# A dense feed-forward with the roles of its two operands exchanged, in a two-block transformer kernel

## The chip, the cores and the metric

One core of one Trainium2 chip runs the whole program in one launch. The metric is device time in microseconds, from the first to the last instruction and what lies around them. All numbers are float32. The core has five engines that run side by side and meet at semaphores: TensorE (PE) multiplies matrices into PSUM, VectorE (DVE) and ScalarE (ACT) do elementwise work, GpSimd (POOL) some more of it, and SyncE (SP) issues most of the DMAs.

## The reference, cut to what matters

The input is one sequence of 256 tokens of width 1024. It goes through a first block (attention and an RWKV group, then a mixture of 32 small experts) and a second block of two layers. The change is in the feed-forward of the first of these two layers:

```
def swiglu(h, w1, w3, w2):
    return (jax.nn.silu(h @ w1) * (h @ w3)) @ w2
...
for i in range(DEPTH_2):                       # 2 layers
    ...                                        # pool and conv mixer, w_out
    x = layer_norm(DEEPNORM_ALPHA * x + mix, ln1_g[i], ln1_b[i])
    if i % 2 == 0:
        f = swiglu(x, dense_w1[j], dense_w3[j], dense_w2[j])       # 1024 -> 2816 -> 1024
    else:
        f = moe_swiglu(x, router_w[j], exp_w1[j], exp_w3[j], exp_w2[j])   # 8 experts, 2 per token
    x = layer_norm(DEEPNORM_ALPHA * x + f, ln2_g[i], ln2_b[i])
    x = x + jax.nn.sigmoid(x @ ple_gate_w[i]) * (p[i] @ ple_w[i])
```

## The kernel before

Tokens stand in two tiles of 128 rows (TT = 2). Each engine has one instruction stream, written out by hand in program order; the lists in STEPS name the points at which an engine raises its semaphore, and `ba`, `bd` and `bp` turn such a name into a wait on ACT's, DVE's or PE's list.

Weights stream through `ring`, seven places of 2 MB. SP issues one piece after another in a fixed order; piece n waits until `used`, a count that PE raises as it finishes with pieces, shows piece n-7 read. So the order of the pieces must be the order in which PE finishes with them. `has(n)` is PE's wait for piece n. After the dense pieces come those of the per-layer gate (PLE: ple_w and two of ple_gate_w), of the second layer's mixer and of its experts.

A matmul loads a block of 128 columns as the stationary side and moves up to 512 columns of the other operand past it. In the trace a float32 matmul is two pairs of a weight load (LDWEIGHTS) and a MATMUL instruction, so all counts of the trace are twice those of the code; a transposing matmul is one pair.

The dense feed-forward cuts the 2816 middle columns into units of 512, 512, 512, 512, 512 and 256 (UD). For a unit u and a token tile t:

- L1540: w1, 8 matmuls. The stationary side is a 128-token block of `xT` (the input, transposed before), the weights move, 512 columns at a time. The result has tokens in rows.
- L1547: w3, the same, into PSUM bank 2.
- L958 on ACT: silu of the w1 result into `hs`. L2178 on DVE: the product with the w3 result into `hh`.
- L1528: four transposes of `hh` into PSUM bank 3, since the next product needs the middle columns in rows. L2181 on DVE: copy into `hT`.
- L1518: w2, 8 matmuls per tile: `hT` is stationary and w2 moves, 512 columns at a time, summed over all units in PSUM banks 4 to 7.

The order on PE is: w1 of (u, t), the transposes of the step before, w3 of (u, t), w2 of the step before. After the last step the transposes and w2 of (5, 1) stand alone. Then DVE adds the sum to x (L2185) and normalizes, and the gate stage follows (L1468, L1479, L1292, L1497), and the second mixer, which begins with L1400. That stage, and the first mixer before, already use the other form: weight columns are stationary and the whole `xT`, 256 tokens wide, moves (L1400 and, in the first block, L1023).

The eight experts of the second layer run as a loop on PE with two bodies, one for experts with few tokens (two halves of the array) and one for the others; a value read at run time picks one.

Of the kernel before, what the change touches and what calls it, by code (L numbers as in the profile page):

```python
# [10 lines left out]
ALU = mybir.AluOpType  # L11
ACT = mybir.ActivationFunctionType
# [3 lines left out]
P = 128  # L16
D = 1024
S = 256
TT = S // P
KD = D // P  # L20
# [56 lines left out]
class Steps:  # L77
# [12 lines left out]
    def __call__(self, name):  # L90
# [71 lines left out]
    ],  # L162
# [13 lines left out]
def build(nc, x, positions, g_mix, w_in, g_cq, w_uq, g_ckv, w_uk, w_uv, g_qn, g_kn, g_mla_out, rw_mu, rw_w0, rw_w2,  # L176
# [4 lines left out]
    with ExitStack() as ctx:  # L181
# [13 lines left out]
        xT = sb("xT", [P, KD, S])  # L195
        work = sb("work", [P, 14368])
        c_sb = sb("c_sb", [P, TT, C_W])
        ident = sb("ident", [P, P])
# [14 lines left out]
        ps = ctx.enter_context(nc.psum_tensor("ps", [P, 8, 512], F32))  # L213

        def cut(base, at, *shape):

            n = int(np.prod(shape))
            v = base[:, at:at + n]
            names = "abcde"[:len(shape)]
            if len(shape) == 1:  # L220
                return v
            return v.rearrange(f"p ({' '.join(names)}) -> p {' '.join(names)}", **dict(zip(names[1:], shape[1:])))
# [86 lines left out]
        mean, var = tiny(16), tiny(16)  # L309
# [14 lines left out]
        hs = cut(work, 1792, 2, 512)  # L324
        hh = cut(work, 2816, 2, 512)
        hT = cut(work, 3840, 4, P)
        yg = cut(work, 4352, D)
        RT = 7480
        at_rt = [RT]

# [10 lines left out]
        diffs, w2 = rt(2, 5), rt(2, 2)  # L341
# [16 lines left out]
        up = cut(work, 0, NPC, 16 + S)  # L358
# [49 lines left out]
        def place(n):  # L408

            at = (n + 1) % PLACES * PLACE  # L410
            return ring[:, at:at + PLACE]
# [4 lines left out]
        def chunked(v, width):  # L416
            return v[:, 0:KD * width].rearrange("p (k n) -> p k n", k=KD)


        def ffn_order(units):  # L420

            order = []
            for u in range(units):
                order += [("w1", u), ("w3", u)] + ([("w2", u - 1)] if u else [])
            return order + [("w2", units - 1)]
# [1 line left out]
        MIX = [("in", 1), ("in", 2), ("in", 0), ("pw", 0), ("out", 0), ("out", 1)]  # L427
        PLE = [("ple", 0), ("pg", 0), ("pg", 1)]

        DENSE = [(what, u) for u in range(len(UD)) for what in ("w1", "w3", "w2")]  # L430
        MOE = ffn_order(UNITS)
        MIX0, DENSE0 = 0, len(MIX)
        PLE0 = DENSE0 + len(DENSE)
# [12 lines left out]
        def read_dense(what, u):  # L446
            return read(DENSE0 + DENSE.index((what, u)))

# [8 lines left out]
        def _(sp):  # L457
# [85 lines left out]
            for n, (what, u) in enumerate(DENSE):  # L543
                f0, f = 512 * u, UD[u]
                if what == "w2":
                    src = dense_w2_2[0][f0:f0 + f, :].rearrange("(p c) n -> p c n", p=P)
                else:
                    src = (dense_w1_2 if what == "w1" else dense_w3_2)[0].rearrange("(p k) f -> p k f", k=KD)[:, :, f0:f0 + f]
                piece(DENSE0 + n, src)
# [148 lines left out]
        def _(act):  # L698
# [252 lines left out]
            mixer_act(0)  # L951
            turned_x(0, "ffn 0")
            for u in range(len(UD)):
                for t in range(TT):
                    act.wait_ge(*(bp(f"up {u}") if t == 0 else read_dense("w3", u)))
                    if u > 0:
                        act.wait_ge(*bd(f"hidden {u - 1} {t}"))
                    ba.raise_by(act.activation(hs[:, t, 0:UD[u]], ps[:, t, 0:UD[u]], ACT.Silu), f"silu {u} {t}")  # L958
            tail_act(0)
            mixer_act(1)  # L960

# [31 lines left out]
        def _(pe):  # L993
# [387 lines left out]
            def has(n):  # L1381

                pe.wait_ge(landed[(n + 1) % PLACES], 16 * (n // PLACES + 1))
# [122 lines left out]
            turn_x(x_sb, bp, "xT ffn 0", lambda t: [bd(f"ln1 0 {t}")])  # L1506
            pe.wait_ge(*ba("xT ffn 0 3"))

            def dense_down(u, t):
                n_c = UD[u] // P  # L1510
                n2 = DENSE0 + DENSE.index(("w2", u))
                if t == 0:
                    has(n2)
                pe.wait_ge(*bd(f"hT {u} {t}"))
                w = place(n2)[:, 0:n_c * D].rearrange("p (c n) -> p c n", c=n_c)
                for n in range(2):
                    for c in range(n_c):
                        ins = mm(ps[:, 4 + 2 * t + n, :], hT[:, c, :], w[:, c, n * 512:(n + 1) * 512], start=(u == 0 and c == 0),  # L1518
                                 stop=(u == len(UD) - 1 and c == n_c - 1))
                if t == 1:  # L1520
                    ins.then_inc(used, 1)

            def dense_turn(u, t):
                n_c = UD[u] // P
                pe.wait_ge(*bd(f"hidden {u} {t}"))
                v = hh[:, t, 0:UD[u]].rearrange("p (q c) -> p c q", c=n_c)
                for c in range(n_c):
                    ins = turn_(ps[:, 3, c * P:(c + 1) * P], v[:, c, :], ident[:, :])  # L1528
                bp.raise_by(ins, f"hT {u} {t}")

            before_ = None
            for u in range(len(UD)):
                n1, n3 = DENSE0 + DENSE.index(("w1", u)), DENSE0 + DENSE.index(("w3", u))
                has(n1)
                has(n3)
                for t in range(TT):
                    if u > 0:
                        pe.wait_ge(*ba(f"silu {u - 1} {t}"))
                    for k in range(KD):
                        ins = mm(ps[:, t, 0:UD[u]], xT[:, k, t * P:(t + 1) * P], chunked(place(n1), UD[u])[:, k, :],  # L1540
                                 start=(k == 0), stop=(k == KD - 1))
                    if t == 1:
                        ins.then_inc(used, 1)
                    if before_:
                        dense_turn(*before_)
                    for k in range(KD):
                        ins = mm(ps[:, 2, 0:UD[u]], xT[:, k, t * P:(t + 1) * P], chunked(place(n3), UD[u])[:, k, :],  # L1547
                                 start=(k == 0), stop=(k == KD - 1))
                    if t == 0:
                        bp.raise_by(ins, f"up {u}")  # L1550
                    else:
                        ins.then_inc(used, 1)
                    if before_:
                        dense_down(*before_)
                    before_ = (u, t)
            dense_turn(*before_)
            dense_down(*before_)
            ple_pe(0, PLE0, False)
            mixer_pe(1, MIX1)

# [130 lines left out]
        def _(dve):  # L1691
# [10 lines left out]
            def mark(stage, ins, name):  # L1702

                stage.raise_by(ins, name)
                dve.wait_ge(*stage(name))
# [467 lines left out]
            mixer_dve(0)  # L2173

            for u in range(len(UD)):
                for t in range(TT):
                    dve.wait_ge(*ba(f"silu {u} {t}"))
                    mark(bd, tt(hh[:, t, 0:UD[u]], hs[:, t, 0:UD[u]], ps[:, 2, 0:UD[u]], ALU.mult), f"hidden {u} {t}")  # L2178
                    dve.wait_ge(*bp(f"hT {u} {t}"))
                    n_c = UD[u] // P  # L2180
                    mark(bd, cp(hT[:, 0:n_c, :].rearrange("p c s -> p (c s)"), ps[:, 3, 0:UD[u]]), f"hT {u} {t}")  # L2181
            dve.wait_ge(*read_dense("w2", len(UD) - 1))
            for t in range(TT):
                x_t = x_sb[:, t, :].rearrange("p (b n) -> p b n", b=2)
# [111 lines left out]
```

## Time and profile before

| | |
|---|---|
| median of 3 runs | 2221.1 us (2213.69 to 2238.5) |
| profiled execution, its own time | 2220.31 us |
| its span | 2218.5 us |
| PE busy | 1920.7 us, 87% of the span |
| DVE, ACT, POOL busy | 506.2, 240.7, 65.5 us |
| mean granted TensorE clock | 0.94 of full speed |
| HBM read | 543.50 MB, 245 GB/s over the span |

The profiled execution lies 0.8 us under the median, and 1.8 us of it lies outside the span. Times in the trace are from the span's start.

### The profile page before, as it was taken

To read this page: it belongs to the slowest core of one execution; us is meant where nothing else is said; L and a number is where in the kernel's file an instruction comes from. 1 tells how busy PE (TensorE), PEld (TensorE's weight loads), DVE (VectorE), ACT (ScalarE), POOL (GpSimd) and SP (SyncE) were. 2 spreads that over 40 slices of the span, in tenths; PEclk is the share of its full clock that TensorE was granted. 3 is DMA by queue.
4 is the path that set the end of the run, shared out by engine and by line. 5 is a ranking of instruction groups with operands and counts; after the bars stand their busy time and mean duration, and the time that the engine had idled before them with its cause. 6 is when DMAs were issued, how large, how long until landed. Compare 5 with 4: busy or idle time off the path is not lost.

```text
span 2218.5 us, 23585 instructions
## 1 busy us (share of the span) xinstructions
PE 1920.7 (87%) x10059; PEld 1121.5 (51%) x10060; DVE 506.2 (23%) x828; ACT 240.7 (11%) x418; POOL 65.5 (3%) x141
## 2 busy tenths in 40 slices
PE   3967867777878999989779999999799999998877
PEld 2846754554664444548454454455444445544443
DVE  1356621111472000037321000011111001110102
ACT  1242101111211000012110000000000000010001
POOL 3000100000020000001000000000000000000000
PEclk9977869999988999999879999999899999999999
DMA  7040128999733351454127867879999888999990
GB/s 269 1 192 2 40 81 360 402 389 413 276 114 114 114 189 57 168 187 147 38 92 283 296 243 287 294 281 405 393 404 396 313 295 323 397 402 398 402 362 19
DMA packets 169984, 545.75 MB, mean 246 GB/s; under 512 B 6521, under 2 KB 9698, under 8 KB 148146
## 3 DMA queue, kind: packets, MB, share of 16 engines
q1 hardware_dynamic: 166640, 538.33, 63.7%
q0 software_dynamic: 1664, 5.05, 0.7%
q8 instruction: 65, 1.06, 0.2%
q10 hardware_dynamic: 1602, 1.19, 0.2%
q14 instruction: 13, 0.11, 0.0%
HBM read 543.50 MB, written 1.05 MB: 245 GB/s over the span
## 4 chain that ended last, share of the span: by engine, by line
PE 71%; DVE 13%; DMA 8%; issue 3%; ACT 2%; SPq 2%; ACTq 0%; DVEq 0%
PE ps L1611 20%; DMA ring<-in_exp_w 7%; PE ps L1629 7%; DVE work L2137 5%; PE ps L1635 4%; PE ps L1540 4%; PE ps L1518 3%; PE ps L1547 3%; PE ps L1573 3%; PE ps L1328 3%; PE ps L1342 3%; PE ps L1497 3%; PE ps L1455 2%; PE ps L1023 2%; SPq L564 2%
## 5 line engine op out<-in xcount | busy, mean ns | idle before, releaser
L1611 PE MATMUL ps<-ring,work 128*64 128x256 f32 (+1 forms) x2912 | 563.5, 438 | 33.1 <-DMA ring<-in_exp_w 21.6
L1611 PEld LDWEIGHTS ps<-ring,work 128*64 128x64 f32 (+1 forms) x2912 | 282.4, 148 | 298.4 <-issue 183.7
L1635 PE MATMUL ps<-ring,work 128*64 128x512 f32 x560 | 136.0, 631 | 18.9 <-DMA ring<-in_exp_w 10.0
L1629 PE MATMUL ps<-ring,work 128*128 128x512 f32 x336 | 147.8, 593 | 4.6 <-DVE work L2241 4.6
L2241 DVE COPY work<-ps 128x512 f32<-128x512 f32 x56 | 38.7, 690 | 430.6 <-PE ps L1619 430.6
L2235 DVE TENSOR_TENSOR work<-work,ps 128x512 f32<-128x512 f32 x56 | 38.5, 688 | 341.6 <-PE ps L1611 341.6
L975 ACT ACTIVATE work<-ps 128x512 f32<-128x512 f32 x56 | 33.5, 598 | 682.1 <-PE ps L1611 682.1
L1629 PEld LDWEIGHTS ps<-ring,work 128*128 128x128 f32 x336 | 63.6, 190 | 84.0 <-issue 84.0
L2137 DVE SCALAR_TENSOR_TENSOR work<-work,c_sb 128x256 f32<-128x256 f32 x180 | 98.8, 549 | 6.4
L1635 PEld LDWEIGHTS ps<-ring,work 128*64 128x64 f32 x560 | 41.6, 144 | 94.0 <-issue 75.5
L1400 PE MATMUL ps<-xT,ring 128*128 128x256 f32 x384 | 85.8, 387 | 1.1 <-ACT xT L898 1.1
L1400 PEld LDWEIGHTS ps<-xT,ring 128*128 128x128 f32 x384 | 74.6, 195 | 12.4 <-issue 1.9
L1540 PE MATMUL ps<-ring,xT 128*128 128x512 f32 (+1 forms) x192 | 80.2, 572 | 0.7 <-ACT xT L898 0.7
L1328 PE MATMUL ps<-work,xn 128*128 128x128 f32 x256 | 63.3, 425 | 20.1 <-DVE work L2072 20.1
L1518 PE MATMUL ps<-ring,work 128*128 128x512 f32 x176 | 77.6, 593 | 0.6 <-DVE work L2181 0.6
L1547 PE MATMUL ps<-ring,xT 128*128 128x512 f32 (+1 forms) x192 | 77.6, 557 | 0.0
L1573 PE MATMUL ps<-work,xn 128*128 128x128 f32 x288 | 70.3, 405 | 5.8 <-DVE work L2217 5.8
L1573 PEld LDWEIGHTS ps<-work,xn 128*128 128x128 f32 x288 | 69.5, 334 | 11.0 <-DVE work L2217 5.9
L1328 PEld LDWEIGHTS ps<-work,xn 128*128 128x128 f32 x256 | 61.8, 336 | 26.1 <-DVE work L2072 26.1
L1342 PE MATMUL ps<-ring,work 128*32 128x256 f32 x1024 | 58.6, 387 | 11.2 <-DVE work L2076 11.2
L1540 PEld LDWEIGHTS ps<-ring,xT 128*128 128x128 f32 x192 | 37.3, 195 | 42.2 <-issue 40.4
L1497 PE MATMUL ps<-ring,xT 128*128 128x512 f32 x128 | 56.0, 595 | 2.9 <-ACT xT L898 2.9
(463 smaller groups left out, 1682.2 us busy)
## 6 DMA issues: line engine op xcount, KB each, us to landing
ring<-in_exp_w SPq DMA_DIRECT2D x168, 2048.0 KB, 14.5
ring<-in_w_gate SPq DMA_DIRECT2D x32, 1024.0 KB, 8.6
ring<-in_w_up SPq DMA_DIRECT2D x32, 1024.0 KB, 15.4
ring<-in_w_down SPq DMA_DIRECT2D x32, 1024.0 KB, 17.9
ring<-in_dense_w SPq DMA_DIRECT2D x15, 2048.0 KB, 8.1
ring<-in_w_in SPq DMA_DIRECT2D x6, 2048.0 KB, 11.0
ring<-in_w_in SPq DMA_DIRECT2D x8, 1104.0 KB, 16.8
ring<-in_w_out SPq DMA_DIRECT2D x4, 2048.0 KB, 15.4
```

Source lines behind the costliest of these rows:

```text
L1328: ins = mm(ps[:, k // 4, (k % 4) * P:(k % 4 + 1) * P], by8(xn[:, t, :])[:, k, :], ga_sel[:, t, :], start=(t == 0), stop=(t == TT - 1))
L1342: ins = mm(ps[32 * j:32 * j + 32, 2, n * F1:(n + 1) * F1], xg[:, k, 32 * j:32 * j + 32], ring[:, at + k * F1:at + (k + 1) * F1], start=(k ...
L1400: ins = mm(ps[:, bank, half * S:(half + 1) * S], w[:, k, i * P:(i + 1) * P], xT[:, k, :], start=(k == 0), stop=(k == KD - 1))
L1497: ins = mm(ps[:, 2 * t + n, :], xT[:, k, t * P:(t + 1) * P], wg[k // 4][:, k % 4, n * 512:(n + 1) * 512], start=(k == 0), stop=(k == KD - 1))
L1518: ins = mm(ps[:, 4 + 2 * t + n, :], hT[:, c, :], w[:, c, n * 512:(n + 1) * 512], start=(u == 0 and c == 0), stop=(u == len(UD) - 1 and c = ...
L1540: ins = mm(ps[:, t, 0:UD[u]], xT[:, k, t * P:(t + 1) * P], chunked(place(n1), UD[u])[:, k, :], start=(k == 0), stop=(k == KD - 1))
L1547: ins = mm(ps[:, 2, 0:UD[u]], xT[:, k, t * P:(t + 1) * P], chunked(place(n3), UD[u])[:, k, :], start=(k == 0), stop=(k == KD - 1))
L1573: ins = mm(ps[:, 6 + k // 4, (k % 4) * P:(k % 4 + 1) * P], by8(xn[:, t, :])[:, k, :], ga_sel[:, t, :], start=(t == 0), stop=(t == TT - 1))
L1611: ins = mm(ps[cols_j, bank, 0:fh], xg[:, k, cols_j], w[:, k, :, n_c * j:n_c * (j + 1)], start=(k == 0), stop=(k == KD - 1), **tile)
L1629: ins = mm(ps[:, 4 + n, :], hT[:, c, :], w[:, c, n * 512:(n + 1) * 512], start=(first and c == 0), stop=(final and c == 3))
L1635: ins = mm(ps[rows_n, 4 + n, :], hT[:, c % 2, side(c // 2)[0]], w[:, c, n * 512:(n + 1) * 512], start=(first and c == 0), stop=(final and ...
L2137: ins = stt(yv[:, j, :], vp[:, j, tap:tap + S], cw[:, tap, j:j + 1], yv[:, j, :], ALU.mult, ALU.add)
```

## The change

The first two products of the dense feed-forward are turned round. For each chunk of 128 middle columns, the 128 columns of w1 (then of w3) are the stationary side and `xT`, all 256 tokens, moves. The result has the middle columns in rows and is what w2's product takes as its stationary side, after silu and the product. So the transposes on PE and the copies on DVE are gone. ACT and DVE work once per unit, on both tiles together (up to 1024 elements per partition). The PSUM banks are 0 and 1 for w1, 2 and 3 for w3, 4 to 7 for the sum. `hT_d` has two buffers, and w2 of unit u-1 comes after w3 of unit u. The pieces are therefore read in another order, that of `ffn_order` (w1 0, w3 0, w1 1, w3 1, w2 0, w1 2, w3 2, w2 1, and so on, w2 5 last), and w2's rows are laid out as (c p) instead of (p c): a partition now gets four separate rows of 4 KB where it had 16 KB in one run.

```
-        DENSE = [(what, u) for u in range(len(UD)) for what in ("w1", "w3", "w2")]
+        DENSE = ffn_order(len(UD))
...
-                    src = dense_w2_2[0][f0:f0 + f, :].rearrange("(p c) n -> p c n", p=P)
+                    src = dense_w2_2[0][f0:f0 + f, :].rearrange("(c p) n -> p c n", p=P)
...
-                for t in range(TT):
-                    act.wait_ge(*(bp(f"up {u}") if t == 0 else read_dense("w3", u)))
-                    if u > 0:
-                        act.wait_ge(*bd(f"hidden {u - 1} {t}"))
-                    ba.raise_by(act.activation(hs[:, t, 0:UD[u]], ps[:, t, 0:UD[u]], ACT.Silu), f"silu {u} {t}")
+                act.wait_ge(*read_dense("w1", u))
+                if u > 0:
+                    act.wait_ge(*bd(f"hidden {u - 1}"))
+                n_b = UD[u] // 256
+                ba.raise_by(act.activation(hs_d[:, 0:2 * UD[u]].rearrange("p (b n) -> p b n", b=n_b), ps[:, 0:n_b, :], ACT.Silu),
+                            f"silu {u} u")
...
+            def dense_up(what, u, b):
+                n = DENSE0 + DENSE.index((what, u))
+                has(n)
+                w = chunked(place(n), UD[u])
+                for c in range(UD[u] // P):
+                    for k in range(KD):
+                        ins = mm(ps[:, b + c // 2, (c % 2) * S:(c % 2 + 1) * S], w[:, k, c * P:(c + 1) * P], xT[:, k, :],
+                                 start=(k == 0), stop=(k == KD - 1))
+                ins.then_inc(used, 1)
+
+            def dense_down(u):
+                ...
+                has(n2)
+                pe.wait_ge(*bd(f"hidden {u}"))
+                for t in range(TT):
+                    for n in range(2):
+                        for c in range(n_c):
+                            ins = mm(ps[:, 4 + 2 * t + n, :], hT_d[:, u % 2, c, t * P:(t + 1) * P], w[:, c, n * 512:(n + 1) * 512],
+                                     start=(u == 0 and c == 0), stop=(u == len(UD) - 1 and c == n_c - 1))
+                ins.then_inc(used, 1)
...
             for u in range(len(UD)):
...
+                if u > 0:
+                    pe.wait_ge(*ba(f"silu {u - 1} u"))
+                dense_up("w1", u, 0)
+                if u > 0:
+                    pe.wait_ge(*bd(f"hidden {u - 1}"))
+                dense_up("w3", u, 2)
+                if u > 0:
+                    dense_down(u - 1)
+            dense_down(len(UD) - 1)
...
+                dve.wait_ge(*ba(f"silu {u} u"))
+                dve.wait_ge(*read_dense("w3", u))
+                n_b = UD[u] // 256
+                mark(bd, tt(hT_d[:, u % 2, 0:2 * n_b, :].rearrange("p (b c) s -> p b (c s)", b=n_b),
+                            hs_d[:, 0:2 * UD[u]].rearrange("p (b n) -> p b n", b=n_b), ps[:, 2:2 + n_b, :], ALU.mult),
+                     f"hidden {u}")
```

## Rows read from the trace of the kernel before

**Rows 1.** The page: the span, and the chain that ended last, by engine

```profile
span 2218.5 us, 23585 instructions
PE 1920.7 (87%) x10059; PEld 1121.5 (51%) x10060; DVE 506.2 (23%) x828; ACT 240.7 (11%) x418; POOL 65.5 (3%) x141
PE 71%; DVE 13%; DMA 8%; issue 3%; ACT 2%; SPq 2%; ACTq 0%; DVEq 0%
```

**Rows 2.** Busy time by stretch: us, each engine (instructions), granted clock, DMA share, GB/s

```profile
710.01:945.60 235.59, 235.00 (x604) 112.61 (x604) 15.49 (x24) 9.28 (x14) 0.00 (x0) 0.99 0.37 134
768.60:941.30 172.70, 172.70 (x461) 84.84 (x459) 11.62 (x18) 6.23 (x10) 0.00 (x0) 1.00 0.40 142
```

**Rows 3.** The timeline of PE: start, length, line; the stage's first units

```profile
710.01 9.73 PE L1540 MATMUL ps<-ring,xT 128*128 128x512 f32 x16 [0.69 <-ACT xT L898]
719.58 7.03 PE L1547 MATMUL ps<-ring,xT 128*128 128x512 f32 x16
726.45 7.03 PE L1540 MATMUL ps<-ring,xT 128*128 128x512 f32 x16
733.32 0.63 PE L1528 MATMUL ps<-ident,work 128*128 128x128 f32 x4
733.79 7.03 PE L1547 MATMUL ps<-ring,xT 128*128 128x512 f32 x16
740.66 7.03 PE L1518 MATMUL ps<-ring,work 128*128 128x512 f32 x16
```

**Rows 4.** The timeline of PE at the stage's end

```profile
916.11 3.62 PE L1540 MATMUL ps<-ring,xT 128*128 128x256 f32 x16
919.56 0.64 PE L1528 MATMUL ps<-ident,work 128*128 128x128 f32 x4
...
933.81 0.39 PE L1528 MATMUL ps<-ident,work 128*128 128x128 f32 x2
934.03 3.62 PE L1547 MATMUL ps<-ring,xT 128*128 128x256 f32 x16
...
940.92 0.39 PE L1528 MATMUL ps<-ident,work 128*128 128x128 f32 x2
941.90 3.70 PE L1518 MATMUL ps<-ring,work 128*128 128x512 f32 x8 [0.59 <-DVE work L2181]
948.34 0.63 PE L1468 MATMUL ps<-ident,st 128*128 128x128 f32 x4 [2.74 <-DVE x_sb L2185]
```

**Rows 5.** The timeline of PE in the first and the second mixer

```profile
582.87 41.68 PE L1400 MATMUL ps<-xT,ring 128*128 128x256 f32 x192 [0.58 <-ACT xT L898]
624.39 7.07 PE L1419 MATMUL ps<-work,xn 128*128 128x256 f32 x32
996.95 44.17 PE L1400 MATMUL ps<-xT,ring 128*128 128x256 f32 x192 [0.57 <-ACT xT L898]
```

**Rows 6.** One line's instructions (L1400): ns min, median, max

```profile
L1400 PEld LDWEIGHTS ps<-xT,ring x384: 187/190/337, 582.8 to 1040.5; 128*128 128x128 f32 x192
```

**Rows 7.** Busy time by stretch, 128x256 matmuls under load

```profile
582.90:624.40 41.50, 41.50 (x193) 36.54 (x194) 31.53 (x66) 11.71 (x36) 0.00 (x0) 1.00 0.57 221
```

**Rows 8.** Lines of DVE and ACT: ns min, median, max of one instruction

```profile
L2185 DVE SCALAR_TENSOR_TENSOR x_sb<-x_sb,ps x2: 1221/1222/1222, 945.7 to 947.0; 128x1024 f32<-128x1024 f32 x2
L948 ACT ACTIVATE work<-ps x4: 1024/1024/1026, 978.2 to 2211.9; 128x1024 f32<-128x1024 f32 x4
```

**Rows 9.** DMA issues on the page: KB each, us to landing

```profile
ring<-in_dense_w SPq DMA_DIRECT2D x15, 2048.0 KB, 8.1
ring<-in_w_in SPq DMA_DIRECT2D x6, 2048.0 KB, 11.0
ring<-in_w_out SPq DMA_DIRECT2D x4, 2048.0 KB, 15.4
```

**Rows 10.** The timeline of PE at two turns of the expert loop

```profile
1566.01 6.62 PE L1635 MATMUL ps<-ring,work 128*64 128x512 f32 x16 [1.78 <-DVE work L2241]
1582.76 8.82 PE L1611 MATMUL ps<-ring,work 128*64 128x256 f32 x64 [10.13 <-issue]
...
1934.65 6.62 PE L1635 MATMUL ps<-ring,work 128*64 128x512 f32 x16 [1.78 <-DVE work L2241]
1941.09 5.17 PE L1611 MATMUL ps<-ring,work 128*64 128x256 f32 x44
```

**Rows 11.** The instruction queue: packets, MB, from 710 to 946 us

```profile
q8 instruction: 5, 0.08, 0.1%
```

**Rows 12.** The instruction queue from 1566 to 1583 us

```profile
q8 instruction: 4, 0.07, 2.5%
```

More of the change, by code:

```diff
@@ L327, in build @@
         yg = cut(work, 4352, D)
+        hs_d = cut(work, 1792, 4 * S)
+        hT_d = cut(work, 2816, 2, 4, S)
         RT = 7480
@@ L1507, in _ @@
             pe.wait_ge(*ba("xT ffn 0 3"))
-            def dense_down(u, t):
+            def dense_up(what, u, b):
[7 more added lines that the diff above has]
+                ins.then_inc(used, 1)
@@ L1510, in dense_down @@
+            def dense_down(u):
                 n_c = UD[u] // P
                 n2 = DENSE0 + DENSE.index(("w2", u))
-                if t == 0:
-                    has(n2)
-                pe.wait_ge(*bd(f"hT {u} {t}"))
+                has(n2)
+                pe.wait_ge(*bd(f"hidden {u}"))
                 w = place(n2)[:, 0:n_c * D].rearrange("p (c n) -> p c n", c=n_c)
[L1516 to L1531, printed above, removed]
-            for u in range(len(UD)):
[L1533 to L1555, printed above, removed]
@@ L1556, in _ @@
-            dense_turn(*before_)
-            dense_down(*before_)
+                for t in range(TT):
[4 more added lines that the diff above has]
+                ins.then_inc(used, 1)
+            for u in range(len(UD)):
+                if u > 0:
[6 more added lines that the diff above has]
+                    dense_down(u - 1)
@@ L2175, in _ @@
             for u in range(len(UD)):
[L2176 to L2181, printed above, removed]
+                dve.wait_ge(*ba(f"silu {u} u"))
[4 more added lines that the diff above has]
+                     f"hidden {u}")
             dve.wait_ge(*read_dense("w2", len(UD) - 1))
```

12 rows, old and new, of the table STEPS are left out of this document.

## The prediction, made before the changed kernel ran

> **What bounds the kernel now.** I read the page first: PE is busy 87% of the span, and 71% of the chain that ended last is PE's [rows 1]. That says where to look, not what an edit is worth, so next came the stretch of the dense feed-forward. It goes from the first w1 matmul at 710.01 us to the end of the last w2 matmul at 945.60 us, 235.59 us, and PE is busy in 235.00 us of it; the DMA engines are busy in 0.37 of their time, DVE in 15.49 us [rows 2]. In the timeline the reader is to see that one group starts where the one before it left off, and to count by starts, not by lengths: matmuls overlap, so the 7.03 us of a group are longer than what it takes from the stream. 16 instructions of 128x512 start over 6.87 us, from 719.58 to 726.45, so 429.4 ns each; four transposes take 0.47 us, from 733.32 to 733.79 [rows 3]. The stage is PE's instruction stream and little else. Whatever leaves that stream shortens the kernel, and whatever enters it lengthens it.
>
> **Removed: the transposes.** Eleven groups stand between two matmul groups. Ten are of four instructions, 0.47 us each: 4.70 us [rows 3]. One is of two, from 933.81 to 934.03: 0.22 us [rows 4]. (The first group of unit 5's stretch, at 919.56, is still of four and is one of the ten.) The twelfth is the last, where nothing is left to lay over the copy on DVE: from 940.92 to 941.90 it costs 0.98 us, of which 0.59 us is PE idle [rows 4]. Together 5.90 us, all on the path. The twelve copies on DVE and the smaller pieces of ACT's and DVE's work lay beside PE's work and give nothing.
>
> **Changed: the shape of w1 and w3.** Five units of 2 x 2 x 16 instructions, 320 of 128x512, become 640 of 128x256. The sixth unit moved 256 columns before and still does: its 64 instructions stay 64. Columns moved in all: the same. What a 128x256 instruction takes stands in two places. In unit 5, from 916.11 to 919.56, 16 take 3.45 us, 215.6 ns each [rows 4]. In the first mixer, in just the form that the change adopts, 192 take 41.52 us, 216.3 ns each [rows 5]. So 640 take 138.0 to 138.4 us, where 320 at 429.4 ns took 137.4 us: 0.6 to 1.0 us more. I take 0.8 us.
>
> **The doubled weight loads.** Each MATMUL has its load; 320 more of them come in. A load takes 190 ns (337 ns at most, in a slow stretch) [rows 6]. In the mixer's stretch they are busy 36.54 of 41.50 us, and still the matmuls start 216 ns apart at a granted clock of 1.00, while the DMA engines are busy in 0.57 of their time [rows 7]. So the load hides under a matmul of 256 columns, with 26 ns to spare, and costs nothing. This is the cover on which the whole change rests; without it, see the second rival. The Trainium skill ("TensorE: Matmul & The Clock Gate", what overlaps and what doesn't, under packing small matmuls) says that a weight load overlaps with matmuls in flight only when its row group differs. All these blocks use all 128 rows, so by that sentence each added load would stand in the stream: at 190 ns a load, by this case's row, the 320 would add 60.8 us and the change would lose. The row of the mixer speaks against it, since 190 ns and the matmul's own time can't stand one after the other in 216 ns (256 columns there take half of what 512 take).
>
> **Moved: the waits.** PE now waits for silu of unit u-1 before w1 of unit u. That silu was let go after w1 of u-1 and takes 1.0 us for 1024 elements (L948, nearest in shape) [rows 8], plus once a table load that stands in ACT's stream now too; w3 of u-1, 13.8 us, lies over it. PE waits for "hidden" of u-1 before w3 of u. DVE starts it when w3 of u-1 is done; it takes about 1.2 us (L2185, 1024 elements from PSUM) [rows 8]. Over it lies w2 of u-2 and w1 of u, at least the 13.8 us of the latter. Behind PE's wait all of PE is queued, so without the cover it would cost about 1.4 us with the semaphores, five times, 7 us. At the end, "hidden" of unit 5 has w2 of unit 4, 13.7 us, over it, and the last w2 starts at once. That is why the 0.59 us go too. The step after the stage is as before: DVE waits for the last w2 matmul, and PE restarts 2.74 us after it [rows 4].
>
> **Moved: the pieces.** Each is issued when the seventh before it is read. The stage needs 34.6 MB in some 230 us, 150 GB/s, and the DMA engines are idle for most of it [rows 2]. A piece of w2 now has rows of 4 KB. Pieces with such rows (w_out) took 15.4 us to land, those of the dense weights 8.1 us at the median, w_in 11.0 us [rows 9]. Six pieces lie ahead of the one being read, at 13.7 us each for PE, so even 15.4 us are hidden; a piece would have to take over 60 us to be late. The pieces behind the stage (the gate's and the second mixer's) go out at most a few us later relative to the stage's end than before; the mixer's first two are wanted only at 996.95 us, 50 us after the end. I put all of it at nothing.
>
> **The sum.** -5.90 + 0.8 = -5.1 us, bounds -5.3 and -4.9. The stage should take 230.5 us. Everything behind it hangs on PE's progress, the transfers of the experts too (they wait for pieces to be read), so the 5.1 us should reach the end. Against the profiled execution: 2220.31 - 5.1 = 2215.2 us; the median of the runs lies 0.8 us above that execution, so 2216 us.
>
> **What the shift disturbs.** Two costs depend on where things fall. First the clock. The stage starts slowly: its first 16 instructions take 9.57 us where the next 16 take 6.87 us, 2.7 us lost, because PE sat idle before [rows 3]. The second mixer needs 44.17 us for what the first does in 41.68 us [rows 5]. Such starts behind the stage (gate, mixer, expert loop) may gain or lose up to 2.7 us each when all moves by 5 us; some cancel, and I allow 3 us to each side. Second, code.
>
> **First rival: the program's layout moves and the expert loop pays otherwise.** At one of the seven turns of the expert loop PE stands idle for 10.13 us and waits for nothing the profile shows, and at another turn, small body to small body as well, there is no gap [rows 10]. In the stretch with the gap the instruction queue carries four packets of 16 KB, beside weights that fill the DMA engines [rows 12]: PE waits for its own code. The dense stage took five such packets for 1208 instructions of PE (604 matmuls and 604 loads) [rows 2, 11], one for some 240. The change adds 320 pairs and takes away 44, 552 instructions, some 2.3 packets, so the loop's code lies otherwise within the packets, and a turn may gain a gap or lose one. Each is worth 10.1 us. One more: -5.1 + 10.1 = +5, 2226 us, slower than before; it decides as soon as one gap is added, as 10.1 is over 5.1. One less: 2206 us. Two or more added, 2236 us and up, need the loads of the loop to collide every time. The Trainium skill ("Runtime: NRT & Kernel Launch", instruction fetch mechanics) says that a taken branch whose target isn't in the buffer forces a fetch before execution goes on, and that a block is 256 instructions. That each turn is such a branch, while six of the seven show no gap, says that most targets are held; by its block size, 552 less some 18 waits is 2 blocks and 22 instructions, which would leave the layout nearly as it is. Chance of a gap more 0.09, of one less 0.08.
>
> **Second rival: the loads don't hide in this stage.** Price: for each ns by which load and gap exceed 216, 640 x 1 ns; if all 190 ns of the 320 added loads stood in the stream, 60.8 us, 2277 us. Against it stands [rows 7], the same shape and operands, under more DMA traffic. Chance 0.02.
>
> **Third rival: the change doesn't shorten the path,** because something other than PE sets the end of the stage. For it to be so, a piece must be late or a wait must be bare; 7 us for the waits would make 2223 us. Nothing in the rows supports it. Chance 0.03.
>
> **How the numbers follow.** Forecast 0.78, centre 2216 us; its own range, with 3 us for the clock and the scatter of the runs (2213.69 to 2238.5 us before, median 2221.1), is 2210 to 2222 us. A gap fewer or more reaches to 2206 and 2226 us, with 1 to 2 us beyond: 2204 to 2228 us. About 1%, 22 us, is what a measurement of this kernel can tell from no change: faster than 2199 us 0.04 (the shift takes away more than one gap), slower than 2243 us 0.04, the rest 0.92.
>
> **What would show it.** In the new profile: no transposes and no copies between 710 and 940 us; w1 and w3 groups of 64 instructions that start 13.8 us apart and of 216 ns each; loads of 190 ns; no idle time of PE inside the stage; its end at about 940.5 us. The gap at an expert's turn tells the first rival, and a pace over 216 ns the second. The prediction is wrong if PE's stream stops somewhere in the stage, or if the total moves by more than the stage does without a changed gap or clock.

## The result, and the profile after

The changed kernel takes 2231.78 us (median of 20 runs, 2229.44 to 2239.32) where the kernel before takes 2216.74 us beside it (20 runs, 2213.56 to 2239.08): a ratio of 1.0052, 95% interval 1.0031 to 1.0073. The medians alone would give 1.0068, but four of the 20 runs of the kernel before lie at 2236 us and above, the other 16 between 2213.56 and 2224.24 us. It is slower by half a percent, and the time lies above the range that was given. The profiled execution took 2237.92 us, the longest but one of its 20, of which the span is 2235.9 us.

The stage that was changed did what it was to do. Busy time of its stretch in the changed kernel, in the columns of [rows 2]:

```profile
717.75:947.80 230.05, 230.05 (x880) 168.73 (x880) 6.80 (x6) 8.24 (x8) 0.00 (x0) 0.99 0.41 143
```

And the timeline of PE in the changed kernel, beside [rows 3, 4]:

```profile
717.75 57.83 PE L1514 MATMUL ps<-xT,ring 128*128 128x256 f32 x256 [0.69 <-ACT xT L896]
775.41 13.90 PE L1527 MATMUL ps<-ring,work 128*128 128x512 f32 x32
789.14 27.79 PE L1514 MATMUL ps<-xT,ring 128*128 128x256 f32 x128
816.77 13.90 PE L1527 MATMUL ps<-ring,work 128*128 128x512 f32 x32
...
927.03 20.76 PE L1527 MATMUL ps<-ring,work 128*128 128x512 f32 x48
950.54 0.63 PE L1467 MATMUL ps<-ident,st 128*128 128x128 f32 x4 [2.74 <-DVE x_sb L2168]
```

The transposes are gone, there is no idle time between the groups, and the stage takes 230.05 us instead of 235.59: 5.5 us less. 128 instructions of 128x256 start over 27.63 us (789.14 to 816.77), 215.9 ns each. The groups of lines in the same stretch (us busy and mean ns of one, then idle time before them):

```profile
L1514 PEld LDWEIGHTS ps<-xT,ring 128*128 128x128 f32 x704 | 135.3, 192 | 21.6 <-issue 1.9 <-ACT xT L896 1.1
...
L2162 DVE TENSOR_TENSOR work<-work,ps 128x1024 f32<-128x1024 f32 (+1 forms) x6 | 6.8, 1133 | 206.2 <-PE ps L1514 206.2
L956 ACT ACTIVATE work<-ps 128x1024 f32<-128x1024 f32 (+1 forms) x6 | 5.7, 953 | 196.2 <-PE ps L1514 196.2
```

Each MATMUL has its load here too, 704 of them of 192 ns, and they lie beside the matmuls. ACT and DVE work six times each in these lines, for 5.7 and 6.8 us in all, and else wait for PE.

The loss is in the expert loop, over 600 us further on, where the diff changes nothing. At four of its seven turns, the four that follow an expert with few tokens, PE now stands idle; before, one turn had such a gap [rows 10]. The timeline of PE in the changed kernel:

```profile
1583.96 10.01 PE L1594 MATMUL ps<-ring,work 128*64 128x256 f32 x64 [9.87 <-issue]
1695.58 15.51 PE L1594 MATMUL ps<-ring,work 128*128 128x512 f32 x32 [11.79 <-issue]
...
1963.76 9.59 PE L1594 MATMUL ps<-ring,work 128*64 128x256 f32 x64 [10.27 <-issue]
2075.09 10.19 PE L1594 MATMUL ps<-ring,work 128*64 128x256 f32 x64 [9.87 <-issue]
```

The list of waits from 1150 to 2250 us puts both sides in one place (us in total, times, longest). The changed kernel:

```profile
PE ps L1594 <- issue: 41.8, 4, 11.8
PE ps L1594 <- DMA ring<-in_exp_w: 7.2, 6, 1.7
PE ps L1618 <- DMA ring<-in_exp_w: 4.3, 5, 1.1
```

The kernel before:

```profile
PE ps L1611 <- DMA ring<-in_exp_w: 21.6, 16, 1.8
PE ps L1611 <- issue: 10.1, 1, 10.1
PE ps L1635 <- DMA ring<-in_exp_w: 10.0, 10, 1.1
```

31.7 us of gaps come in, and 20.1 us of waits for weights go: the transfers run on while PE stands (the DMA engines' share is 1.05 from 1953.5 to 1963.7 us, inside a gap), so a gap in a stretch where the weights are late costs little. That is 11.6 us net. How unlike the three new gaps are, the same places of both timelines show. The kernel before:

```profile
1683.21 14.00 PE L1611 MATMUL ps<-ring,work 128*128 128x512 f32 x32
1843.83 7.48 PE L1611 MATMUL ps<-ring,work 128*64 128x256 f32 x64
...
2154.95 5.35 PE L1635 MATMUL ps<-ring,work 128*64 128x512 f32 x16 [1.78 <-DVE work L2241]
```

The changed kernel:

```profile
1857.71 7.47 PE L1594 MATMUL ps<-ring,work 128*64 128x256 f32 x64
...
2172.24 5.35 PE L1618 MATMUL ps<-ring,work 128*64 128x512 f32 x16 [1.78 <-DVE work L2224]
```

At the end of the first gap, which both kernels have, the changed kernel is 1.20 us behind (1583.96 and 1582.76 us); at the start of the many-token expert 12.37 us (1695.58 and 1683.21); at its end 13.88 us; at the loop's last group 17.29 us. So the one gap ahead of the many-token expert stays in the time whole: no wait for weights is there to be shortened. In the kernel before PE is busy in 159.06 of the 160.60 us from 1683.2 to 1843.8 us, and the DMA engines' share is 0.84. The two later gaps, 20.1 us together, add 3.4 us: they lie where that share is 1.02 to 1.04.

PE also starts more slowly after a gap: the 64 instructions take 9.59 to 10.19 us where after a turn without a gap they take 7.44 to 7.48 us. Busy time by stretch, the changed kernel just behind its first gap, and the kernel before behind a turn without one, shows a granted clock of 0.50, the lower of the two levels, and of 1.00:

```profile
1584.00:1588.00 4.00, 4.00 (x20) 2.28 (x22) 0.00 (x0) 0.00 (x0) 0.00 (x0) 0.50 0.97 373
1941.10:1945.00 3.90, 3.90 (x38) 2.59 (x36) 0.00 (x0) 2.37 (x3) 0.00 (x0) 1.00 1.05 388
```

Of the instruction queue (packets, MB, share) the changed kernel's page says:

```profile
q8 instruction: 92, 1.51, 0.3%
```

and the page of the kernel before:

```profile
q8 instruction: 65, 1.06, 0.2%
```

27 more packets of 16 KB, where the change adds about two packets' worth of code, and 25 of them come between 1100 and 2200 us (56 where there were 31), over the expert loop. That is code fetched again. In the changed kernel's stretch of the gap that ends at 1963.76 us (1951 to 1966 us) there are four of them, as in [rows 12]:

```profile
q8 instruction: 4, 0.07, 2.4%
```

The two profiled spans differ by 17.4 us, more than the medians. 7.7 us of it lie ahead of the changed stage, in code that is the same in both (the stage begins at 717.75 instead of 710.01 us). Over all fourteen profiles of this study the stage begins between 708.8 and 718.0 us, the changed kernel's second profile at 708.82; so this isn't the change's. The stage takes 5.5 us off that, and from its end to the loop's last group the changed kernel falls back by 15.1 us (from 2.20 to 17.29 us behind).

### The profile page after: what moved, and what is told of

It is laid out like the page before. It is cut to its first block, busy times and chain, and to the rows that moved or that the text cites. A ratio compares the mean times of both kernels' runs of the same rounds, so it can differ in the third digit from the quotient of the medians.

```text
span 2235.9 us, 24095 instructions
## 1 busy us (share of the span) xinstructions
PE 1922.4 (86%) x10335; PEld 1181.2 (53%) x10336; DVE 497.6 (22%) x810; ACT 239.5 (11%) x412; POOL 65.3 (3%) x141
## 3 DMA queue, kind: packets, MB, share of 16 engines
HBM read 543.50 MB, written 1.05 MB: 244 GB/s over the span
## 4 chain that ended last, share of the span: by engine, by line
PE 74%; DVE 13%; DMA 6%; issue 4%; ACT 2%; ACTq 0%; SPq 0%; DVEq 0%
PE ps L1594 22%; PE ps L1514 7%; PE ps L1612 6%; PE ps L1618 5%; DMA ring<-in_exp_w 5%; DVE work L2120 5%; PE ps L1527 3%; PE ps L1556 3%; PE ps L1327 3%; PE ps L1341 3%; PE ps L1496 3%; PE ps L1454 2%; PE ps L1022 2%; PE ps L1568 1%; PE ps L1368 1%
## 5 line engine op out<-in xcount | busy, mean ns | idle before, releaser
L1594 PE MATMUL ps<-ring,work 128*64 128x256 f32 (+1 forms) x2912 | 572.5, 444 | 50.4 <-issue 41.8
L1514 PE MATMUL ps<-xT,ring 128*128 128x256 f32 x704 | 155.2, 383 | 0.7 <-ACT xT L896 0.7
L1612 PE MATMUL ps<-ring,work 128*128 128x512 f32 x336 | 147.8, 593 | 4.6 <-DVE work L2224 4.6
L1514 PEld LDWEIGHTS ps<-xT,ring 128*128 128x128 f32 x704 | 135.3, 192 | 21.6 <-issue 1.9
L1399 PE MATMUL ps<-xT,ring 128*128 128x256 f32 x384 | 86.5, 389 | 1.3 <-ACT xT L896 1.3
L1399 PEld LDWEIGHTS ps<-xT,ring 128*128 128x128 f32 x384 | 75.0, 196 | 12.6 <-issue 1.9
L1327 PE MATMUL ps<-work,xn 128*128 128x128 f32 x256 | 63.3, 424 | 20.1 <-DVE work L2055 20.1
L1527 PE MATMUL ps<-ring,work 128*128 128x512 f32 x176 | 76.3, 592 | 0.0
L1454 PE MATMUL ps<-ring,work 128*128 128x512 f32 x128 | 55.4, 593 | 2.3 <-issue 2.3
## 6 DMA issues: line engine op xcount, KB each, us to landing
ring<-in_w_out SPq DMA_DIRECT2D x4, 2048.0 KB, 15.1
```

Source lines behind the costliest of these rows:

```text
L1327: ins = mm(ps[:, k // 4, (k % 4) * P:(k % 4 + 1) * P], by8(xn[:, t, :])[:, k, :], ga_sel[:, t, :], start=(t == 0), stop=(t == TT - 1))
L1399: ins = mm(ps[:, bank, half * S:(half + 1) * S], w[:, k, i * P:(i + 1) * P], xT[:, k, :], start=(k == 0), stop=(k == KD - 1))
L1454: ins = mm(ps[:, 4 + 2 * t + n, :], mT[:, k, t * P:(t + 1) * P], wo[k // 4][:, k % 4, n * 512:(n + 1) * 512], start=(k == 0), stop=(k == K ...
L1514: ins = mm(ps[:, b + c // 2, (c % 2) * S:(c % 2 + 1) * S], w[:, k, c * P:(c + 1) * P], xT[:, k, :], start=(k == 0), stop=(k == KD - 1))
L1527: ins = mm(ps[:, 4 + 2 * t + n, :], hT_d[:, u % 2, c, t * P:(t + 1) * P], w[:, c, n * 512:(n + 1) * 512], start=(u == 0 and c == 0), stop= ...
L1594: ins = mm(ps[cols_j, bank, 0:fh], xg[:, k, cols_j], w[:, k, :, n_c * j:n_c * (j + 1)], start=(k == 0), stop=(k == KD - 1), **tile)
```

## The experiments

**The theory:** the change moves the code of the expert loop, and where it lies sets how often PE must fetch the loop's code again at a turn. **The rival:** the turned stage does something to what follows, by the clock, the order of the pieces or w2's rows of 4 KB.

They can be told apart without touching anything that runs. Counted in PE's part of the built program, from its start (a matmul counts as four instructions, a transposing one as two), the expert loop begins at instruction 8929 before and at 9486 after, 557 later. One branch of PE's program, for a case that these inputs never meet, stands ahead of the dense stage. Never-run matmuls in its body move what follows; the profiles count the same instructions with them as without (23585 in the kernel before, 24095 in the changed one):

```
             with pe.If(extra > 0):
+                for _ in range(m):
+                    mm(ps[:, 7, 0:S], ones[:, :], xT[:, 0, :], start=True, stop=True)
                 with pe.Fori(1, extra + 1) as r:
```

(where four doesn't divide the number, with a transpose, a `pe.drain()` or both more). They move all of PE's code behind the branch, not the loop alone; that the loop's own place is what counts is taken from the gaps, which stand at its turns. No run of this study leaves out or changes a part of the computation.

**Run before_557.** The kernel before, the loop at the place of the changed kernel.

> The kernel before, with 557 more instructions in PE's stream, all in the body of a branch that is never taken, ahead of the dense feed-forward (they are matmuls that never run). The expert loop then begins 557 instructions later, exactly where it begins in the changed kernel; nothing else differs from before. If the loss comes from where the loop's code lies: gaps of 10 to 12 us at four turns of the expert loop instead of one, and a time about 5.6 us over that of the changed kernel (which saves that in the dense stage), 1.007 to 1.009 of before. Rival, the loss comes from something the turned stage does to what follows (clock, DMA order, rows of 4 KB): one gap, and the time of before, 0.998 to 1.002.

2238.42 us, 1.0053 (1.0025 to 1.0081). Four gaps, at the same turns as in the changed kernel; the timeline of PE:

```profile
1581.21 9.47 PE L1614 MATMUL ps<-ring,work 128*64 128x256 f32 x64 [8.69 <-issue]
...
1962.58 9.90 PE L1614 MATMUL ps<-ring,work 128*64 128x256 f32 x64 [9.86 <-issue]
2074.10 8.83 PE L1614 MATMUL ps<-ring,work 128*64 128x256 f32 x64 [11.62 <-issue]
```

(the fourth, before 1692.86 us, is 10.10 us). The old dense stage is in this kernel, with its transposes, so the rival falls: the place alone makes the gaps. The time is less clear. It was to be 1.007 to 1.009 of before and lies at 1.0053, no more than the changed kernel's 1.0052 on another occasion; the 5.5 us of the stage don't show between these two ratios, whose intervals are some 0.005 wide.

**Run after_211.** The changed kernel, the loop three times 256 instructions behind its place before.

> The changed kernel with 211 never-run instructions in the same untaken branch, so that the expert loop begins 768 instructions later than in the kernel before, three times 256. If only the place within a block of 256 counts: one gap of 10 us at a turn of the expert loop, and the saving of the dense stage shows, 5.1 to 5.6 us under before, 0.9975 of it. If the place in a larger buffer counts, other numbers of gaps may come. If the loss has nothing to do with the place: 1.005 of before as in the changed kernel.

2217.03 us, 0.996 (0.9929 to 0.9991): faster than before. Two gaps, 2.52 and 13.20 us, where one of 10 us was expected.

**Run after_1491.** The same, 2048 instructions behind.

> As the run with 211, with 1491 instructions: the expert loop begins 2048 instructions later than in the kernel before. If the place in a buffer of 2048 instructions counts, this one and not the one with 211 gives the gaps of before (one) and 0.9975 of its time; if only the place within 256 counts, both do. If the place does not count: 1.005.

2215.30 us, 0.9971 (0.9937 to 1.0005; the interval just takes in no difference). One gap, of 2.59 us. Both shifts give back the level of before, so the place within 256 instructions does it; that of 2048 isn't needed.

**Run after_128.**

> The changed kernel with 128 never-run instructions in the untaken branch, a place between that of the changed kernel and that of the run with 211. The place theory has no number for it, only that the number of gaps and the time move together: 7 to 10 us of time for each gap outside the stretches where the weights' transfers bound the experts, less inside. Rival, place does not count: 1.005 and four gaps, as in the changed kernel.

2240.90 us, 1.0058 (1.0029 to 1.0088), the slowest of the changed ones. Four gaps, of 14 to 16 us: 58.1 us of them in the list of waits. Here there are 16.3 us more of gaps than in the changed kernel. Whether that costs time can't be told: the medians lie 9.1 us apart, but they were taken on different occasions, on which the kernel before lay 5.3 us apart too, and the ratios, 1.0058 and 1.0052, don't differ clear of their intervals.

**Runs after_64 and after_170.** Two more places between.

> The changed kernel with 64 never-run instructions ahead, bodies in the old order. It lies between the changed kernel (0) and the one with 128, both with four gaps; so four gaps of 10 to 14 us and 1.005 to 1.006 of before. If one gap or none, the place matters in a finer way than by a threshold in the block.

2231.02 us, 1.0042 (1.0017 to 1.0067), four gaps of 9.75 to 11.74 us.

> The changed kernel with 170 never-run instructions ahead, between 128 (four gaps, 1.0058) and 211 (two gaps, 0.996). It narrows where the change from many gaps to few lies. No number is forecast beyond that it is at one of the two levels.

2231.33 us, 1.0041 (1.0015 to 1.0067). Four turns with gaps again, three of them in two parts; the timeline of PE at the first:

```profile
1575.83 1.12 PE L1597 MATMUL ps<-ring,work 128*64 128x256 f32 x4 [9.78 <-issue]
1580.42 9.16 PE L1597 MATMUL ps<-ring,work 128*64 128x256 f32 x60 [3.46 <-issue]
```

With the other runs: the loop's first instruction modulo 256 (counted as above) is 14 in the changed kernel and in before_557, 78, 142 and 184 in the runs with 64, 128 and 170, and 225 in the kernel before and the runs with 211 and 1491. The first five have four turns with gaps, the last three have one or two.

**Runs after_swap and after_swap_128.** The order of the loop's two bodies.

```
-                with pe.If(small_one > 0):
-                    expert_pe(e, 0, 2)
                 with pe.If(small_one < 1):
                     expert_pe(e, 0, 1)
+                with pe.If(small_one > 0):
+                    expert_pe(e, 0, 2)
```

> The changed kernel, with the two bodies of the expert loop in the other order: the one for many tokens first (836 instructions), the one for few tokens (1264) second, next to the loop's end. The loop begins at the same place as in the changed kernel. Theory: at a turn of the loop PE must fetch code because the few-token body and what is read ahead behind it, the loop's end and the loop's start don't lie in its buffer together. With the few-token body next to the end, what is read ahead behind it is the loop's end itself, so turns after a few-token expert should lose their gaps: at most one or two gaps in place of four, a time of 0.996 to 0.999 of before. Rival, the gap comes at each branch back that follows the few-token body, wherever it stands: four gaps and 1.005.

2221.60 us, 0.9997 (0.9973 to 1.0021). The time comes back to that of before, but not as expected: there are still four gaps, 9.14, 3.98, 9.16 and 10.89 us, 33.2 us together instead of 41.8. The one of 3.98 us is that ahead of the many-token expert, 11.79 us in the changed kernel and the one that costs its whole length. The profiled execution took 2228.06 us, the longest of its 12.

> The same with the loop 128 instructions later (never-run ones in the untaken branch), the place that gave four gaps of 14 us and 1.0058 with the old order of the bodies. If the order of the bodies cures it, at most two gaps and under 1.000; if the place rules whatever the order, 1.005.

2213.11 us, 0.9965 (0.9939 to 0.9991), the lowest median of the study. Three gaps, 1.14, 4.21 and 4.24 us, where the old order had four of 14 to 16 us at this place. The timeline of PE:

```profile
1310.98 13.99 PE L1596 MATMUL ps<-ring,work 128*128 128x512 f32 x32 [1.14 <-issue]
1570.28 9.69 PE L1596 MATMUL ps<-ring,work 128*64 128x256 f32 x64 [4.21 <-issue]
...
1935.50 9.69 PE L1596 MATMUL ps<-ring,work 128*64 128x256 f32 x64 [4.24 <-issue]
```

So the order matters as well as the place of the loop's start. The exchange also moves the few-token body, which now begins 837 instructions further on, so order and place of the bodies aren't told apart. My picture of why (what is read ahead behind the few-token body) gave the right sign at both places and too few gaps at both: one or two expected and four seen, at most two expected and three seen. It isn't shown.

**Runs before_256, before_557_again, after_again and after_211_again.** A control, and the main comparison on one chip.

> Control: the kernel before with 256 never-run instructions in the untaken branch. The loop moves by one whole block. If only the place within 256 counts and the padding itself costs nothing: one gap (at most two) and 0.998 to 1.002 of before. If the never-run code costs something by itself: over 1.003.

2224.12 us, 1.0028 (0.9997 to 1.0059), two gaps of 2.69 and 11.55 us. The range of the forecast is missed by a little; the interval takes in no difference, so no cost of the never-run code itself shows.

> The kernel before with 557 never-run instructions once more, now beside the changed kernel on the same chip. The expert loops of the two lie at the same place, so what is left between them is the dense stage: this one should be 5 to 7 us slower than the changed kernel, and 1.006 to 1.008 of before.

2237.49 us, 1.0072 (1.0047 to 1.0097), four gaps.

> The changed kernel once more, on the same chip as the three others of this call: 1.004 to 1.006 of before, four gaps of about 10 us, and 5 to 7 us under the kernel before with 557 never-run instructions.

2229.57 us, 1.0037 (1.0011 to 1.0062; expected were 1.004 to 1.006), four gaps. It is 7.9 us under before_557_again, with the loop at the same place in both. The expectation said 5 to 7 us. Their stages take 230.3 and 235.8 us in the profiles (708.82 to 939.13, and 711.28 to 947.09), 5.5 us apart; the other 2.4 us of the medians have no cause that I can show.

> The changed kernel with 211 never-run instructions once more: the loop lies in its block as in the kernel before, so the saving of the dense stage is left, 5 to 7 us, 0.9970 to 0.9977 of before. The number of gaps varied between one small and two in the two such kernels, so a single profile may show either.

2214.90 us, 0.9973 (0.9945 to 1.0002). This time three gaps, 2.53, 10.30 and 10.07 us, in the same program that showed two in after_211. The timeline of PE:

```profile
1572.08 7.47 PE L1598 MATMUL ps<-ring,work 128*64 128x256 f32 x64 [2.53 <-issue]
1947.57 2.83 PE L1598 MATMUL ps<-ring,work 128*64 128x256 f32 x12 [10.30 <-issue]
2059.94 8.85 PE L1598 MATMUL ps<-ring,work 128*64 128x256 f32 x64 [10.07 <-issue]
```

The profiled execution took 2219.75 us, the longest but one of its 12; that of after_211, with two gaps, lay in the middle of its own (2216.04 us). At this place, then, the gaps come in some executions and not in others. That fits the scatter of the runs: in the last set of runs the kernel before, at 225, ranged from 2210.67 to 2240.14 us (33 runs), before_557_again, at 14, from 2233.31 to 2242.20 (10 runs) and after_again, at 14, from 2227.15 to 2238.62 (12 runs). That the longer executions of before are those with more gaps was only argued: only the profiled executions show their gaps.

These runs, taken beside each other, give both effects by their medians. The place alone (14 against 225) costs 17.6 us in the kernel before (2237.49 and 2219.93 us) and 14.7 us in the changed one (2229.57 and 2214.90 us). The turned stage alone saves 7.9 us at 14 and 5.0 us at 225 (2219.93 and 2214.90 us).

## Why the prediction was wrong

**The sum was right.** -5.1 us for the stage, measured -5.5 us. The load of 190 ns hides under 128x256 in this stage too (215.9 ns from start to start); no wait is bare; the pieces were in time, with w2's rows of 4 KB too (PE waits for none in the stage). The second and the third rival did not come.

**The step that failed is the first rival's weight.** It named the mechanism, the place and the sign (a gap more makes the kernel slower), and gave it 0.09. Two parts of its working were wrong. First, that the shift would "leave the layout nearly as it is". It rested on an estimate of 22 instructions beyond two whole blocks; the built program has 45. Either number is a small part of 256, and the reasoning was that a small shift changes little. But the loop went from 225 to 14, and these two places don't behave alike. Where between places the behaviour changes the trace of before could not say, so 0.09 had nothing to stand on; the runs at 78, 142 and 184 are all bad, so of the five places tried the kernel before stood on the only good one. Second, the price of 10.1 us for each gap, and the words that more would need the loads "to collide every time". At the changed kernel's place the gaps come as a set, at each of the four turns that follow a few-token expert. Three came in, 31.7 us more of gaps in all, and 20.1 us of that were covered by shorter waits for weights. So the count was too low, and one price for all gaps was wrong: the one ahead of the many-token expert brought the kernel 12.7 us further behind (from 1.20 to 13.88 us), the two later ones 3.4 us together. The sum left this term out; it should have had 15.1 us for the way from the stage's end to the loop's last group.

The sum of both: -5.5 + 15.1 = +9.6 us in the two profiled executions. Of the 15.1 us, 11.6 us are the gaps less the waits that they cover; the rest goes with the slower pace behind them. The measured ratio means +11.5 us (of 2216.74), after_again lies 9.6 us over before by the medians, and the first comparison 15.0 us; the kernel before alone has medians of 2216.74 to 2222.06 us on its four occasions, and what is over 9.6 us has no cause that I can show.

**The range** reached to one gap more, 2228 us, and the time lies 4 us above it. It was counted from a median of 2221.1 us of three runs; against the 2216.74 us of 20 the miss is some 8 us.

Of the clock: the 64 instructions behind a gap take up to 10.19 us against 7.47 us, up to 2.7 us lost at a turn, as at the start of the dense stage [rows 3]. This was allowed for as scatter to both sides; with the gaps it fell to one side. Of the code: the Trainium skill ("Runtime: NRT & Kernel Launch", instruction fetch mechanics) calls the instruction memory a FIFO with purely sequential prefetch. In the kernel before, no instruction packet is seen from 1930 to 2140 us, over two turns of the loop: what these turns ran, the few-token body and the loop's ends, some 1270 of the loop's 2108 instructions, was held. The changed kernel has 17 packets in the same stretch. By the rule each of these turns would have to fetch. The measurement decides, and the rule's other half, that a taken branch out of what is held stalls, agrees with the four gaps.

## What to carry to other kernels

Idle time at "issue" behind a branch, with packets on the instruction queue beside it, was code loading here, and it depended on where the loop's code lay. An edit ahead of a loop with a long body can switch it on or off, for more than the edit is worth. Look for it before changing instruction counts, and count the loop's body (here 2108 instructions, two bodies of 1264 and 836, of which turns through the few-token body, some 1270 instructions each, were seen to run without a packet). Price a gap by its stretch: it costs its length where PE's own work is the limit and little where the weights are late. And treat the loop's place as a free parameter: never-run instructions in an untaken branch move it, and the order of the two bodies changes it too. To measure an edit of half a percent, hold the place of what follows fixed, or the comparison measures the place.

## What the runs showed of the hardware that was not expected

- The same changed kernel ranges from 2213 to 2241 us at the median by the place and order of code that does the same work.
- Where the weights' transfers fill the DMA engines, most gaps last 8.6 to 16.2 us, though the packets take only 2.4% of the engines' time in the one stretch shown; some, at 225 and with the bodies exchanged, last 1.1 to 4.2 us, with transfers as dense (a share of 1.05 from 1563 to 1570.7 us, up to the end of the gap of 2.52 us in after_211).
- At 225 the profiles show one to three gaps, two and three of them for one and the same program; at the four other places, with the old order of the bodies, each profile shows four turns with gaps.
- A gap of 11.8 us where PE's work is the limit costs all of it; two of 20.1 us together where the weights are the limit cost 3.4 us.
- Not settled: which rule of the instruction memory makes 14, 78, 142 and 184 bad and 225 good, and why at 142 the exchange of the bodies takes 58 us of gaps down to 10. One reading fits the five places and wasn't tested: cut into blocks of 256 from the program's start, the loop of 2108 instructions lies in nine blocks from the first four and in ten from 225, so the behaviour would change between 196 and 197. It says nothing of the exchange.
